# Weight tile conversions of two attentions' first units moved to units 4 to 6, and the split of one query product moved into the attention

## The reference, cut to what matters

```python
# layer 1 of the first block: 12 query heads, 4 key and value heads, width 64
sc = einsum('bnqhgd,bnkhd->bnhgqk', q, kk) * (HEAD_DIM ** -0.5)
sc = sc - slopes * dist
sc = where(valid, sc, NEG)
p = softmax(concatenate([sc, sink], axis=-1), axis=-1)[..., :-1]
o = einsum('bnhgqk,bnkhd->bnqhgd', p, vv)
...
# second block: selected and windowed branches, 8 heads
out = gc[..., 0:1] * o_c + gc[..., 1:2] * o_s + gc[..., 2:3] * o_w
...
gm = sigmoid(g_merge)
mix = gm[..., :D_MODEL] * (y_a @ w_a_out[l]) + gm[..., D_MODEL:] * (y_b @ w_b_out[l])
```

## Time and profile before

| | us |
|---|---|
| median of 3 runs | 1880.42 |
| lowest and highest | 1880.04, 1880.89 |
| profiled execution, its own time | 1880.36 |
| its span, first to last instruction | 1878.6 |
| TensorE busy | 1862.0 |
| GpSimdE busy | 1015.1 |
| VectorE busy | 862.3 |
| ScalarE busy | 791.5 |
| SWA attention, about | 639 to 777 |
| NSA attention, about | 1268 to 1390 |

### The profile page before, as it was taken

One profiled execution on the slowest core, in us unless ns is written; L12 is line 12 of the kernel. 1 busy time (PEld: TensorE's weight loads), 2 busy tenths in 40 slices (PEclk: granted clock), 3 DMA queues, 4 the chain that ended last, 5 costly groups with the idle time before them and its releaser, 6 DMA issues.

```text
span 1878.6 us, 26672 instructions
## 1 busy us (share of the span) xinstructions
PE 1862.0 (99%) x9075; PEld 1552.6 (83%) x9075; DVE 862.3 (46%) x1744; ACT 791.5 (42%) x1416; POOL 1015.1 (54%) x1340
## 2 busy tenths in 40 slices
PE   8999999999999999999999999999999999999999
PEld 6878888888888888888888888887878888888887
DVE  6777542222236675422222673697752354444200
ACT  6558642323233576432232353647642333233221
POOL 6750465455556654655555564455565456555553
PEclk9999999999999999999999999999999999999999
DMA  6330132332322212332323323221022322332332
GB/s 213 124 107 1 42 100 101 98 95 99 100 91 90 85 40 69 107 100 91 101 91 99 101 79 98 71 75 38 24 95 96 101 90 91 101 99 89 112 101 79
DMA packets 47437, 168.29 MB, mean 90 GB/s; under 512 B 5616, under 2 KB 5872, under 8 KB 47088
## 3 DMA queue, kind: packets, MB, share of 16 engines
q1 hardware_dynamic: 46368, 164.64, 27.2%
q10 hardware_dynamic: 976, 2.39, 0.4%
HBM read 164.13 MB, written 2.10 MB: 88 GB/s over the span
## 4 chain that ended last, share of the span: by engine, by line
PE 93%; DVE 4%; ACT 2%; issue 1%; DMA 0%; POOL 0%; SPq 0%; DVEq 0%; ACTq 0%
PE bank L677 27%; PE bank L679 27%; PE bank L678 27%; PE bank L762 3%; PE bank L808 3%; PE bank L799 2%; PE bank L780 1%; DVE ACC L1483 1%; PE bank L775 0%; ACT WH L1072 0%; DMA X<-x 0%; PE bank L970 0%; PE bank L720 0%; DVE ML_ L1738 0%; DVE XL L1764 0%
## 5 line engine op out<-in xcount | busy, mean ns | idle before, releaser
L588 POOL TENSOR_TENSOR WL<-RAW,WH 128x256 fp32r<-128x256 f32 x1208 | 936.2, 806 | 702.9 <-ACT WH L1072 702.6
L677 PE MATMUL bank<-XH,WH 128*128 128x512 f32 x1311 | 521.4, 398 | 0.8 <-POOL WL L588 0.2
L679 PE MATMUL bank<-XH,WL 128*128 128x512 f32 x1311 | 510.8, 390 | 0.0
L678 PE MATMUL bank<-XL,WH 128*128 128x512 f32 x1311 | 510.6, 389 | 0.0
L1072 ACT ACTIVATE WH<-RAW 128x1024 fp32r<-128x1024 f32 x302 | 316.7, 1051 | 301.3 <-PE bank L679 296.5
L679 PEld LDWEIGHTS bank<-XH,WL 128*128 128x128 f32 x1311 | 246.1, 188 | 51.9
L677 PEld LDWEIGHTS bank<-XH,WH 128*128 128x128 f32 x1311 | 246.3, 188 | 49.6 <-issue 0.7
L678 PEld LDWEIGHTS bank<-XL,WH 128*128 128x128 f32 x1311 | 246.5, 188 | 47.6 <-issue 0.7
L677 PE MATMUL bank<-HH,WH 128*128 128x512 f32 x512 | 199.2, 389 | 0.0
L679 PE MATMUL bank<-HH,WL 128*128 128x512 f32 x512 | 199.2, 389 | 0.0
L678 PE MATMUL bank<-HL,WH 128*128 128x512 f32 x512 | 199.2, 389 | 0.0
(11 more groups left out here) (381 smaller groups left out, 2816.8 us busy)
## 6 DMA issues: line engine op xcount, KB each, us to landing
RAW<-stream SPq DMA_DIRECT2D x302, 512.0 KB, 3.4
out<-X SPq DMA_DIRECT2D x8, 256.0 KB, 4.5
X<-x SPq DMA_DIRECT2D x3, 512.0 KB, 8.3
MEM<-mem SPq DMA_DIRECT2D x1, 1024.0 KB, 11.0
W<-cmp_w ACTq DMA_DIRECT2D x1, 1024.0 KB, 4.6
KT<-KR ACTq DMA_DIRECT2D x1, 768.0 KB, 8.9
CT<-consts SPq DMA_DIRECT2D x1, 513.0 KB, 12.2
X<-x SPq DMA_DIRECT2D x2, 256.0 KB, 3.3
```

Source lines behind the costliest of these rows:

```text
L588: ins = pool.tensor_tensor(WL[:, slot, c], RAW[:, slot, c], WH[:, slot, c].bitcast(F32), ALU.subtract)
L677: pe.matmul(dst, lhs[0], rhs[0], start=start, stop=False)
L678: pe.matmul(dst, lhs[0], rhs[1], start=False, stop=False)
L679: return pe.matmul(dst, lhs[1], rhs[0], start=False, stop=stop)
```

## The change

TensorE's and SyncE's instructions stay as they are. The edits:

- SWA, ScalarE: the conversion of one weight tile (that of three outputs ahead) goes from step 2 to step 6.
- SWA, GpSimdE: the low half of that tile goes from ahead of `bias(2)` to behind it.
- SWA, VectorE: the low half of query tile 1 (heads 2 and 3) goes from ahead of the attention to step 5. Since `PROB1` is used by then, the tile is kept in `POSF1`, and ScalarE reads it there.
- NSA, ScalarE: the conversions of two gate tiles go from step 1 to step 4.
- NSA, GpSimdE: the four pieces of the first of these tiles (gate output 1) go from behind units 2 to 5 to behind units 4 to 7.
- NSA, VectorE: the draining of gate output 0 goes from step 8 to step 9.

```diff
--- before.py
+++ after.py
@@ -651,10 +651,13 @@
             lo_parts(converted("wo0"), early)
             pool.wait_ge(signal("dist_done"), 1)
             for h in range(NH):
+                if h == 2 * EARLY_Q - 2:
+                    bias(h)
                 if h >= 2 * EARLY_Q - 2 and h % 2 == 0:
                     lo_part(early, early % RING)
                     early += 1
-                bias(h)
+                if h != 2 * EARLY_Q - 2:
+                    bias(h)
             late = plan.out_tile[plan.out0["in1"] + 13] + AHEAD + 1
             for n in range(early, late):
                 lo_part(n, n % RING)
@@ -665,8 +668,9 @@
             for i in range(len(ATTENTION["nsa"][0])):
                 normalise("nsa", i)
                 for j in range(2 * EARLY_GATES):
-                    if 2 <= i - GATE_AT[KD * j] < 6:
-                        lo_piece(tile + j, (tile + j) % RING, i - GATE_AT[KD * j] - 2)
+                    first = GATE_AT[KD * j] + (2 if j else 4)
+                    if first <= i < first + 4:
+                        lo_piece(tile + j, (tile + j) % RING, i - first)
             lo_parts(tile + 2 * EARLY_GATES, plan.tiles)
 
 
@@ -1319,14 +1323,14 @@
                     split_k((drained, in1 + o), PROB1[:, o - 1, :], K1H[:, 2 * (o - 1):2 * o, :])
                 elif o >= 7:
                     split_q((drained, in1 + o), PROB1[:, o - 5, :], Q1[:, 2 * (o - 7):2 * (o - 6), :])
-            split_q((drained, in1 + 6 + EARLY_Q), PROB1[:, 1 + EARLY_Q, :], Q1[:, 2 * EARLY_Q - 2:2 * EARLY_Q, :])
+            split_q((drained, in1 + 6 + EARLY_Q), POSF1, Q1[:, 2 * EARLY_Q - 2:2 * EARLY_Q, :])
 
             def late_query(tile):
                 dst = Q1[:, 2 * tile:2 * tile + 2, :] if tile < 6 else QX[:, 2 * tile - NH:2 * tile - NH + 2, :]
                 return lambda: split_q((drained, in1 + 7 + tile), QX1[tile % 2], dst)
 
             late = {8 * tile - 7 - 2 * (tile == EARLY_Q): late_query(tile) for tile in range(EARLY_Q, 8)}
-            late |= {8 * tile - 14: lambda o=in1 + 6 + tile: keep_ahead(o) for tile in range(EARLY_Q, 8)}
+            late |= {8 * tile - 14 + 4 * (tile == EARLY_Q): lambda o=in1 + 6 + tile: keep_ahead(o) for tile in range(EARLY_Q, 8)}
             attention("swa", late)
             act.dma_start(W1[:], cmp_w1).then_inc(signal("w_cmp_in"), 16)
             act.dma_start(W2[:], cmp_w2).then_inc(signal("w_cmp_in"), 16)
@@ -1425,7 +1429,7 @@
                     act.activation(PCT[:, g, :], bank[:], ACT.Copy).then_inc(signal("cmp_copied"), 1)
 
             late = {5: cmp_copy}
-            late |= {GATE_AT[KD * j] + 1: lambda o=plan.out0["gates"] + j: keep_ahead(o, 2) for j in range(2 * EARLY_GATES)}
+            late |= {GATE_AT[KD * j] + (1 if j else 4): lambda o=plan.out0["gates"] + j: keep_ahead(o, 2) for j in range(2 * EARLY_GATES)}
             attention("nsa", late)
             merged = merge_outs()
             for at, m in enumerate(MERGE_ORDER):
@@ -1851,11 +1855,11 @@
             key_low(1)
             for m in range(EARLY_Q + 1):
                 if m < EARLY_Q:
-                    split_value(in1 + 6 + m, s1 + 2 + m, PROB1[:, 2 + m, :], RBC, -SCALE)
+                    split_value(in1 + 6 + m, s1 + 2 + m, PROB1[:, 2 + m, :] if m < EARLY_Q - 1 else POSF1, RBC, -SCALE)
                 if m < 3:
                     dve.wait_ge(drained, in1 + 5 + m)
                     dve.memset(BANK[SCORES["swa"][m]][:, 2 * P:2 * P + 1], 0.0).then_inc(signal("column_zeroed"), 1)
-                if m:
+                if 0 < m < EARLY_Q:
                     split_lo_q(s1 + 1 + m, PROB1[:, 1 + m, :], Q1[:, 2 * m - 2:2 * m, :])
 
             def late_query(tile):
@@ -1873,6 +1877,7 @@
 
             late = {8 * tile - 8 - 2 * (tile == EARLY_Q): late_query(tile) for tile in range(EARLY_Q, 8)}
             late |= {8 * tile - 5 - 2 * (tile == EARLY_Q): late_query_lo(tile) for tile in range(EARLY_Q, 8)}
+            late[5] = lambda: split_lo_q(s1 + 1 + EARLY_Q, POSF1, Q1[:, 2 * EARLY_Q - 2:2 * EARLY_Q, :])
             attention("swa", late)
             output_projection("wo1", "mlp1", "mlp1")
             dve.tensor_tensor(GF[:], GV[:, GAIN["final"]:GAIN["final"] + KD], GV[:, GAIN["norm1"]:GAIN["norm1"] + KD],
@@ -2076,7 +2081,7 @@
                 return step
 
             late = {1: lambda: cmp_weights(0), 2: lambda: cmp_weights(1)}
-            late |= {max(GATE_AT[KD * j + KD - 1] + 1, 2 * NT * (j + 1)): early_gate(j)
+            late |= {max(GATE_AT[KD * j + KD - 1] + 1, 2 * NT * (j + 1) + 1): early_gate(j)
                      for j in range(2 * EARLY_GATES)}
             attention("nsa", late)
```

## The result

| | before | after |
|---|---|---|
| median of 5 runs | 1880.04 | 1887.57 |
| lowest and highest | 1878.64, 1880.89 | 1886.74, 1888.97 |
| profiled execution, its own time | 1880.36 | 1887.15 |
| its span | 1878.6 | 1885.3 |

The ratio is 1.0045, with an interval of 1.0033 to 1.0056 (the two medians alone give 1.0040). The direction was as predicted; the time lies 0.6 us above the range.

The account below looks back on a forecast made before the run. TensorE, with work in 99% of the span, was taken as the bound, so only its standing still counted. Waits of 2.1 (sliding window) and 3.05 (second block) summed to 5.15, giving 1885.5; range 1882.3 to 1887.0.

Parts of the forecast that it names:

- the exponential of unit 4: Second block, ScalarE: starts at 1275.4 behind the two moved weight tiles, 1.26 us later than before.
- the turn of unit 2: Second block, TensorE: needs the first copy of the compressed scores, so goes from 1275.25 to 1276.5.
- the late product: Second block, TensorE: waits for the second gate tile's low half, starting at 1282.15 instead of 1279.12, +3.05 us.
- GpSimdE's row of scalings and pieces: Second block: from about 1278.0 GpSimdE works without pause through units 5 to 7, 4.2 us less 0.15; tile ready at 1282.05.
- Sliding window, waits: Sliding-window attention: TensorE's turn of unit 4 slips by 2.1 us, bounds 1.8 to 2.4.
- unit 5's bias: Sliding window, VectorE: starts at 645.7 instead of 644.02, behind the two moved low-half rows (+1.4) and 0.3 of collision.
- the collision of the scaling: Sliding window: VectorE's scaling of unit 2 beside GpSimdE's bias table of head 2 adds 0 to 0.5 us, taken as 0.3.
- the copy of unit 2: Sliding window, ScalarE: starts at 649.7 in place of 647.59, +2.1 us, and holds up TensorE's turn of unit 4.
- the turn of unit 3: Sliding window, TensorE: waits for ScalarE's copy of unit 1 and slips by 2.65 us, from 645.48 to 648.1.
- no further wait of TensorE grows: Sliding window, after the turn of unit 4: ScalarE has room (it waited 1.31 us before at 650.73) and catches up.
- The clock drops: Rival: TensorE's pauses of up to 2.3 us lower its clock, costing 2.5 us more, 1888.0; chance 0.10.
- The other rivals: Not slower, waits in both places shorten, 1878.0, chance 0.08; one place only costs, 1883.5 or 1882.5, chance 0.14.

Follow-up runs that it names:

- the filled kernel: The whole change plus 18 extra matmuls with unread results where TensorE only waits, in both attentions; 1886.12 (ratio 1.0034).
- the kernel with the split alone: The kernel before with only the low half of query tile 1 made in step 5 on VectorE, kept in `POSF1`; 1882.27 (1.0013).
- the tile alone: The kernel before with only the sliding window's weight tile moved, on ScalarE to step 6 and on GpSimdE behind head 2's bias table; 1881.32 (1.0007).
- the kernel with the second half alone: The kernel before with only the edits to the second block's attention; 1884.51 (1.0026).

## Where the prediction was right, and where it failed

**Second block, waits: right.** The window's extra time moves everything behind it; corrected by these 2.21, the exponential of unit 4 starts at 1277.60 - 2.21 = 1275.39 (predicted 1275.4), the turn of unit 2 at 1276.49 (1276.5), and the late product at 1282.15 (1282.15). GpSimdE's row of scalings and pieces is the one worked out from the earlier trace rows.

**Sliding window, waits: right in the sum, incomplete in the list.** Corrected by 0.79, unit 5's bias starts at 645.86 (predicted 645.7; the collision of the scaling took 0.40 where I took 0.3) and the copy of unit 2 at 649.82 (649.7). The wait before the turn of unit 3 came as two, 1.22 at the scores of unit 8 and 1.50 at the turn: I had not followed those scores, which need unit 5's bias. I also called the turn of unit 3 at 645.48 a wait of before; its row has none, and the sum did not use it. What was missing is the collision further down. I wrote that behind unit 4 "no further wait of TensorE grows", and had looked at ScalarE's slack only; GpSimdE's table of head 3, which stood at 647.39 and now comes 3.4 us later, falls on VectorE's low half of tile 2 and brings a wait of 0.72 at full clock, 0.91 by the stage.

**The step that failed** is that the sum had no term for TensorE's clock. "The clock drops" stood beside it as the third rival, at a chance of 0.10 and outside the range. The runs showed in its place 0.83 us lost to the lower clock in the window (the turn of unit 4 in after against the filled kernel) and 1.57 in the second block. The argument against it was that a wait of 0.85 us had passed at full clock in before. But after puts 1.22 and 1.50 into little over three microseconds, and 1.31, 0.28, 0.21, 0.15 and 2.09 into seven. In the window the clock fell in each of the four profiles that have its edits and no fillers, and in the kernel with the split alone, with waits of 0.28, 1.78 and 0.56; with the tile alone (1.41 and 0.27) it did not. In the second block it fell in two of the four profiles that have those edits and no fillers, and in the first filled kernel ahead of its fillers there. Nor is the place the same: in after it fell behind the wait of 2.09, in the kernel with the second half alone and in the filled one already ahead of it, behind 1.31, 0.28 and 0.21. What decides this in one execution and not in another stays open.

The Trainium skill (TensorE: Matmul & The Clock Gate, section HAM oscillation — how this bites in real kernels), which the prediction named beside this rival, tells of waits between bursts of matmuls that put the array back to half rate. The outcome here agrees (0.93 and 0.83), but the waits in that section are longer than any in these two places (at most 2.09 us), so by it alone the drop was not to be expected, and the prediction's "by that rule this rival would hold" went further than the section does.

The rival's price, 2.5, came close to 0.83 + 1.57 = 2.4, but that is in part luck: it was read from one long stretch at the program's start, while here two shorter falls add up, and in another execution of the same kernel the second did not come. Forecast and clock in both places give 1880.04 + 2.12 + 0.83 + 3.03 + 1.57 = 1887.6, beside 1887.57 measured; with executions of this kernel 3.3 us apart, a match this close is chance too.

**The other rivals** did not come: no stage of the changed kernel got shorter, and both places cost their waits.

## What to carry to other kernels

When a change makes a full TensorE wait in several places a few microseconds apart, the clock is a term of the sum and not a remark: price half speed for the matmuls behind as a chance of its own, let the range reach it, and take several executions. When an order on GpSimdE is changed, follow each of its instructions down the program and look what two-input work of VectorE falls beside it, also behind the place of the edit. And measure by stages between rows that all kernels share: it showed costs of about 1 us which the whole time hid, and one that covered another.

## What the runs showed of the hardware

- The granted clock after the same waits is not the same in each execution: the second block of the changed kernel took 30.04 at 0.83 and 28.50 at 1.00, with equal waits. A single profile can catch either. The nine executions took 1885.65 to 1888.97 at mean clocks of 0.995 to 0.997; the 82 executions of before on record beside the experiments took 1878.24 to 1880.93, a spread not much smaller, but none had a mean clock under 0.998.
- VectorE's subtraction of 64x512 took 0.69 us alone, 1.43 beside a GpSimdE table of 1.12, and 1.02 to 1.11 beside GpSimdE's own subtractions.
- Ten extra matmuls kept the clock at 1.00 in the window, and cost nothing: corrected for the start, the turn of unit 3 stands at 648.29 with them and without.
